# A gated delta rule with the two heads of a block as one 128x128 diagonal tile

## What is computed

```
def gated_delta_rule(q, k, v, beta, log_a):        # chunks of 64 tokens
    g = cumsum(log_a)                              # in the chunk
    a_mat = einsum("bhnid,bhnjd->bhnij", k_beta, k) * decay_strict
    t_inv = triangular_solve(eye + a_mat, eye)     # 64x64, lower
    u = t_inv @ (v * beta)
    w = t_inv @ (k_beta * exp(g))
    p = einsum("bhnid,bhnjd->bhnij", q, k) * decay_causal
    def step(state, xs):                           # chunk after chunk
        v_new = u_c - w_c @ state
        o = q_c @ state + p_c @ v_new
        state = state * exp(gl) + k_c.T @ v_new
```

## Time and profile before

| | before |
|---|---|
| median of 3 runs | 2759.77 us (2758.72 to 2763.18) |
| the profiled execution, its time | 2764.25 us |
| its span, first to last instruction | 2762.5 us |
| mean granted TensorE clock | 0.983 of full speed |
| TensorE busy | 2626.0 us (95%) |
| VectorE busy | 1878.4 us (68%) |
| ScalarE busy | 1232.8 us (45%) |
| GpSimd busy | 405.4 us (15%) |

### The profile page before, as it was taken

The page is one execution under the profiler, slowest core; times in us unless marked ns, Lnnn a source line. Parts: engine busy times, 40 slices in busy tenths (PEclk is TensorE's granted clock), DMA queues, the critical chain, the costliest instruction groups (busy, mean ns, idle before and its releaser), DMA issues.

```text
span 2762.5 us, 38277 instructions
## 1 busy us (share of the span) xinstructions
PE 2626.0 (95%) x15010; PEld 2122.1 (77%) x15010; DVE 1878.4 (68%) x2273; ACT 1232.8 (45%) x2308; POOL 405.4 (15%) x354
## 2 busy tenths in 40 slices
PE   7999998999899999999999999899997999999997
PEld 6887566877788887888778888655776888888885
DVE  3466554673877778888964664589646655578889
ACT  3323565333777763333553334467317433333332
POOL 4322001448200000000300000001374000000002
PEclk9999999999999999999999999899999999999998
DMA  3210000004265655222423223501353232342323
GB/s 136 54 38 13 11 6 24 3 32 183 93 205 188 212 171 193 105 92 107 152 83 116 77 77 122 187 28 35 97 189 125 89 122 92 122 173 101 122 107 122
DMA packets 213484, 290.43 MB, mean 105 GB/s; under 512 B 16551, under 2 KB 143806, under 8 KB 213310
## 3 DMA queue, kind: packets, MB, share of 16 engines
q1 hardware_dynamic: 195918, 227.75, 24.8%
q10 hardware_dynamic: 17392, 60.30, 5.5%
HBM read 220.91 MB, written 67.11 MB: 104 GB/s over the span
## 4 chain that ended last, share of the span: by engine, by line
PE 77%; DVE 11%; ACT 4%; POOL 3%; issue 3%; DMA 2%; SPq 0%; ACTq 0%; DVEq 0%; POOLq 0%
PE ps L1727 7%; PE ps L1728 7%; PE ps L1729 7%; PE ps L1782 6%; PE ps L1784 6%; PE ps L1783 6%; PE ps L1865 4%; PE ps L1866 4%; PE ps L1867 4%; PE ps L1530 2%; PE ps L1436 2%; PE ps L1309 1%; PE ps L1311 1%; PE ps L1310 1%; PE ps L1458 1%
## 5 line engine op out<-in xcount | busy, mean ns | idle before, releaser
L1782 PE MATMUL ps<-down_t_hi,down_s_hi 128*128 128x512 f32 x896 | 349.4, 390 | 3.9 <-DVE acc L3328 2.2
L1784 PE MATMUL ps<-down_t_hi,down_s_lo 128*128 128x512 f32 x896 | 348.6, 389 | 0.0
L1783 PE MATMUL ps<-down_t_lo,down_s_hi 128*128 128x512 f32 x896 | 348.6, 389 | 0.0
L2470 ACT CAST down_s_hi<-down_a 128x2048 fp32r<-128x2048 f32 x56 | 107.3, 1915 | 368.8 <-PE ps L1784 327.1
L1142 POOL TENSOR_SCALAR mean_sq<-ssq 128x1 f32<-128x1 f32 x64 | 37.2, 581 | 1295.8 <-ACT squares_junk_ffn L2018 1246.0
L1727 PE MATMUL ps<-act_hi,up_hi 128*128 128x512 f32 (+1 forms) x544 | 205.7, 378 | 6.1 <-issue 3.6
L1728 PE MATMUL ps<-act_lo,up_hi 128*128 128x512 f32 (+1 forms) x544 | 204.9, 377 | 0.0
L1729 PE MATMUL ps<-act_hi,up_lo 128*128 128x512 f32 (+1 forms) x544 | 204.8, 376 | 0.0
L1782 PEld LDWEIGHTS ps<-down_t_hi,down_s_hi 128*128 128x128 f32 x896 | 168.2, 188 | 41.9 <-issue 7.5
L1784 PEld LDWEIGHTS ps<-down_t_hi,down_s_lo 128*128 128x128 f32 x896 | 168.2, 188 | 35.3
L1783 PEld LDWEIGHTS ps<-down_t_lo,down_s_hi 128*128 128x128 f32 x896 | 168.2, 188 | 34.6
(11 more groups left out here) (382 smaller groups left out, 6460.8 us busy)
## 6 DMA issues: line engine op xcount, KB each, us to landing
down_a<-hid_spill SPq DMA_DIRECT2D x32, 1024.0 KB, 6.6
hid_spill<-up_hid ACTq DMA_DIRECT2D x30, 1024.0 KB, 6.0
w_ada<-in_w_ada SPq DMA_DIRECT2D x48, 512.0 KB, 3.8
up_raw<-in_w_in SPq DMA_DIRECT2D x18, 1024.0 KB, 5.2
raw<-in_w_out SPq DMA_DIRECT2D x32, 512.0 KB, 3.7
up_raw<-in_w_up SPq DMA_DIRECT2D x16, 1024.0 KB, 5.3
down_b<-in_w_down SPq DMA_DIRECT2D x16, 1024.0 KB, 6.7
up_raw<-in_w_mlp_in SPq DMA_DIRECT2D x16, 1024.0 KB, 5.3
```

The source lines that it names most:

```text
L1782: pe.matmul(out, ops["s_hi"][:, k, cols], ops["t_hi"][:, k, :], start=first, stop=False, skip_group_check=True)
L1783: pe.matmul(out, ops["s_hi"][:, k, cols], ops["t_lo"][:, k, :], start=False, stop=False, skip_group_check=True)
L1784: mm = pe.matmul(out, ops["s_lo"][:, k, cols], ops["t_hi"][:, k, :], start=False, stop=last, skip_group_check=True)
```

## The change

The level matrices, the copied Y, `p_T` and `k_dec` are kept as diagonal tiles: [128, 4 blocks, 2, 64] (for `k_dec` two tiles, one for each g), in which the half of the partitions of head g is filled in the columns of g alone and the rest is zero. A matmul with such a tile as weights, 128x128, does both heads at once (`diagonal_products`: 4 matmuls in place of 8). The zeros are written once, by memsets on VectorE before the first level; each later use writes only the filled parts, so what wrote 128 partitions in one instruction now does it in two of 64 (the copy of Y, `p_T`, `k_dec`) or, on GpSimd, in two whole ones with a mask for each g over only the odd blocks of the level, half of the columns. Each level has its own `a_level` tiles. The subtraction of levels 1 to 4 now goes to `t_inv_T`, and the transpose that makes `t_inv` stands right behind it. The constants grow by five masks of 64 columns. The squares for the norm go to `o_normed` in place of a tile of their own.

```diff
@@ constants
+        level = ((k[:, :CHUNK] // s) % 2 == 1) & (r % CHUNK // s == k[:, :CHUNK] // s - 1)
+        for g in range(2 if n else 1):
+            c[:, level_mask(n, g):level_mask(n, g) + CHUNK] = level & (r // CHUNK == g) if n else level
@@ GpSimd, gdn_levels
-                    pool.tensor_tensor(m_s[(n + i) % 2][a][:], a_t[i % 2][a][:], each_block(C_LEVEL + n * CHUNK), ALU.mult)\
-                        .then_inc(sem("level_done"), 1)
+                    if i == 0:
+                        pool.wait_ge(sem("diag_zeroed"), n if n == 1 else n + 1)
+                    for g in range(2):
+                        mask = odd_blocks(consts[:, level_mask(n, g):level_mask(n, g) + CHUNK].unsqueeze(1), n)
+                        ins = pool.tensor_tensor(odd_blocks(m_s[n - 1][a][:, :, g, :], n), odd_blocks(a_t[i % 2][a][:], n),
+                                                 mask.broadcast_to([P, GDN_BLOCKS, CHUNK // LEVELS[n] // 2, LEVELS[n]]), ALU.mult)
+                    ins.then_inc(sem("level_done"), 1)
@@ TensorE
+            def diagonal_products(bank, lhs, rhs, signal):
+                for n in range(GDN_BLOCKS):
+                    mm = pe.matmul(ps[:, bank, n * CHUNK:(n + 1) * CHUNK], lhs[:, n, :, :].rearrange("p g t -> p (g t)"),
+                                   rhs[:, n, :], start=True, stop=True)
+                mm.then_inc(sem(signal), 1)
@@ TensorE, gdn_state_update
-                        for g, m in ((0, 0), (1, 1), (0, 1), (1, 0)):
-                            mm = pe.matmul(ps[gdn_half(m), 5 + g, h * P:(h + 1) * P], k_d[a][gdn_half(g), 2 * h + c, gdn_half(m)],
-                                           v_n[gdn_half(g), h, :], start=True, stop=True)
+                        for g in range(2):
+                            mm = pe.matmul(ps[:, 5 + g, h * P:(h + 1) * P], k_d[a][g][:, 2 * h + c, :], v_n[:, h, :],
+                                           start=True, stop=True)
...
-                    for g in range(2):
-                        n = 2 * h + c
-                        mm = pe.matmul(ps[gdn_half(g), 7, n * P:(n + 1) * P], p_t[a][gdn_half(g), n, :],
-                                       v_n[gdn_half(g), h, :], start=True, stop=True)
+                    n = 2 * h + c
+                    mm = pe.matmul(ps[:, 7, n * P:(n + 1) * P], p_t[a][:, n, :, :].rearrange("p g t -> p (g t)"), v_n[:, h, :],
+                                   start=True, stop=True)
@@ TensorE, gdn_pair
-                            pe.wait_ge(sem("t_done"), 8 * i + (2 * (n - 2) + a + 1))
-                        block_products(a, lambda h, c, rows, b: m_s[(n + i) % 2][a][rows, b, :],
-                                       lambda h, c, rows, b: t_f[f_old][a][rows, b, :], CHUNK, "y_prod")
+                            pe.wait_ge(sem("tr_done"), 8 * i + (2 * (n - 2) + a + 1))
+                        diagonal_products(a, m_s[n - 1][a], t_f[f_old][a], "y_prod")
...
+                        diagonal_products(a if last else 2 + a, y_s[a], t_r[old][a], "zt_prod" if last else "z_prod")
@@ ScalarE, gdn_pair
-                        act.copy(y_s[a][:], block_bank(a)).then_inc(sem("y_done"), 1)
+                        if i == 0 and n == 1:
+                            act.wait_ge(sem("diag_zeroed"), 2)
+                        for g in range(2):
+                            ins = act.copy(y_s[a][gdn_half(g), :, g, :], block_bank(a)[gdn_half(g), :, :])
+                        ins.then_inc(sem("y_done"), 1)
@@ VectorE, gdn_scaled
-                dve.tensor_tensor(p_t[a][:], block_bank(6), e_d[i % 2][a][:], ALU.mult).then_inc(sem("gdn_turn_read"), 1)
+                for g in range(2):
+                    ins = dve.tensor_tensor(p_t[a][gdn_half(g), :, g, :], block_bank(6)[gdn_half(g), :, :],
+                                            e_d[i % 2][a][gdn_half(g), :, :], ALU.mult)
+                ins.then_inc(sem("gdn_turn_read"), 1)
...
-                dve.tensor_tensor(k_d[a][:], bank(4), by_block(G_CD, t), ALU.mult).then_inc(sem("gdn_turn_read"), 1)
+                for g in range(2):
+                    ins = dve.tensor_tensor(k_d[a][g][gdn_half(g), :, :], bank(4)[gdn_half(g), :, :],
+                                            by_block(G_CD, t)[gdn_half(g), :, :], ALU.mult)
+                ins.then_inc(sem("gdn_turn_read"), 1)
@@ VectorE, before the first pair
             dve.memset(state[0][:], 0.0).then_inc(sem("state_done"), 1)
+            gdn_system(0, 0)
+            zeroed(m_s[0])
+            gdn_first_turn(0, 0)
+            gdn_system(0, 1)
+            gdn_first_turn(0, 1)
+            zeroed(y_s)
+            for n in range(1, 5):
+                zeroed(m_s[n])
+            dve.memset(p_t[0][:], 0.0)
+            dve.memset(p_t[1][:], 0.0)
             for a in range(2):
-                gdn_system(0, a)
-                gdn_first_turn(0, a)
+                for g in range(2):
+                    dve.memset(k_d[a][g][:], 0.0)
```

More of the change, by code:

```diff
@@ L354, with level_mask @@
 C_LEVEL = 640
-C_ID64 = C_LEVEL + CHUNK * len(LEVELS)
+C_ID64 = C_LEVEL + CHUNK * (2 * len(LEVELS) - 1)
 C_CSUM64 = C_ID64 + CHUNK
+def level_mask(n, g):
+    return C_LEVEL + CHUNK * (2 * n - 1 + g if n else 0)
 C_KEYCAP = C_CSUM64 + CHUNK
@@ L613, in blocks, with diagonal @@
             return [sb(f"{name}{a}", kb + a, [P, GDN_BLOCKS, CHUNK]) for a in range(2)]
[L615 to L618, removed]
+        k_w, v_b, u_s, w_t, o_i = (tile_pair(n, kb) for n, kb in (
+            ("k_w", 25), ("v_b", 29), ("u", 41), ("w_T", 45), ("o_inter", 53)))
+        k_d = [[head_tile(f"k_dec{a}_{g}", kb) for g, kb in enumerate(kbs)] for a, kbs in enumerate(((49, 51), (189.25, 194)))]
+        def diagonal(name, kb):
+            return sb(name, kb, [P, GDN_BLOCKS, 2, CHUNK])
+        e_d, a_t, t_f = ([blocks(f"{n}{x}_", kb + 2 * x) for x in range(2)]
+                         for n, kb in (("decay", 89), ("a_T", 93), ("t_inv", 101)))
+        m_s = [[diagonal(f"a_level{n + 1}_{a}", kb) for a, kb in enumerate(kbs)]
+               for n, kbs in enumerate(((33, 35), (37, 39), (97, 99), (67, 69), (71, 185)))]
         t_r = [blocks(f"t_inv_T{x}_", 105 + 2 * x) for x in range(3)]
-        y_s, p_t = blocks("level_y", 111), blocks("p_T", 113)
+        y_s = [diagonal(f"level_y{a}", 111 + 2 * a) for a in range(2)]
+        p_t = [diagonal(f"p_T{a}", 199 + 2 * a) for a in range(2)]
         def t_home(i):
@@ L631, in two_blocks @@
         v_n = sb("v_new", 119, [P, 2, P])
-        s_dec, o_s, o_sq, o_n = (head_tile(n, kb) for n, kb in (
-            ("state_dec", 187), ("o_tok", 192), ("o_sq", 194), ("o_normed", 196)))
+        s_dec, o_s, o_n = (head_tile(n, kb) for n, kb in (("state_dec", 187), ("o_tok", 192), ("o_normed", 196)))
         e_last = sb("exp_g_last", 204.5, [P, NT, 2, GDN_HEADS])
@@ L1177, in each_block, with odd_blocks @@
                 return consts[:, mask:mask + CHUNK].unsqueeze(1).broadcast_to([P, GDN_BLOCKS, CHUNK])
+            def odd_blocks(block, n):
+                return block.rearrange("p b (q two s) -> p b q two s", two=2, s=LEVELS[n])[:, :, :, 1, :]
             def gdn_levels(i, n):
@@ L2210, in gdn_squares @@
                 for n in range(GDN_BLOCKS):
-                    ins = act.activation(o_sq[:, n, :], o_s[:, n, :], ACT.Square, accum_out=o_ss[:, n:n + 1])
+                    ins = act.activation(o_n[:, n, :], o_s[:, n, :], ACT.Square, accum_out=o_ss[:, n:n + 1])
                 ins.then_inc(sem("o_ss_done"), 1)
@@ L2976, in gdn_level_turn @@
                 dve.wait_ge(sem("t_done"), 8 * i + (2 * (n - 1) + a + 1))
-                dve.transpose(t_r[t_slot(i, n)][a][:].rearrange("p n t -> p (n t)"), t_f[(n + i) % 2][a][:].rearrange("p n t -> p (n t)"))\
+                dve.transpose(t_f[(n + i) % 2][a][:].rearrange("p n t -> p (n t)"), t_r[t_slot(i, n)][a][:].rearrange("p n t -> p (n t)"))\
                     .then_inc(sem("tr_done"), 1)
@@ L3028, in gdn_pair @@
                 for n in range(1, len(LEVELS)):
-                    old, new, f_new, last = t_slot(i, n - 1), t_slot(i, n), (n + i) % 2, n == len(LEVELS) - 1
+                    old, new, last = t_slot(i, n - 1), t_slot(i, n), n == len(LEVELS) - 1
                     if i and not last:
@@ L3046, in gdn_pair @@
                             dve.wait_ge(sem("z_prod"), 8 * i + (2 * (n - 1) + a + 1))
-                            dve.tensor_tensor(t_f[f_new][a][:], t_f[1 - f_new][a][:], block_bank(2 + a), ALU.subtract)\
+                            dve.tensor_tensor(t_r[new][a][:], t_r[old][a][:], block_bank(2 + a), ALU.subtract)\
                                 .then_inc(sem("t_done"), 1)
+                            gdn_level_turn(i, n, a)
                     for a in range(2):
-                        if not last:
-                            gdn_level_turn(i, n, a)
-                        elif more:
+                        if last and more:
                             gdn_first_turn(i + 1, a)
@@ L3059, in gdn_pair, with zeroed @@
```

(10 more changed lines are left out.)

10 lines of the change are left out of this document (removed).

## The result

The changed kernel takes 2819.31 us, the median of 4 runs (2816.7 to 2834.32), and the kernel before on the same chip 2760.64 us (2758.72 to 2763.18, 4 runs). The ratio is 1.0221, with a 95% interval of 1.0206 to 1.0235: slower, as forecast, but by 59 us and not by 37, and above the range.

What follows compares the result with a forecast made beforehand. TensorE was taken to bound the later pairs, a chain of dependent work the first. Terms 25.0 + 6.5 + 2.0 + 2.2 + 0.7 + 0.4 = 36.8 us gave 2797 us against the median; eight-in-ten range 2780 to 2814.

Steps and rivals of the forecast that it cites:

- the last of the first pair: First pair's low clock: one level at 1.2 GHz, +2.8 us, taken as +2, bounds 0 and 8.
- the chain shows; or the clock stays low: Rival, 17%: later pairs' copies or subtraction and transpose uncovered, or first pair's clock low; 2803 to 2812, say 2807 us.
- my 106: Price in ns of a joined 128x128 pass, set by its weight load, with the stream overlapped.
- levels +7.7 us a pair for +6.4: Levels 1 to 4 of a later pair: level products 1.25 and state update 0.36 a level, +6.4 us on TensorE.
- The end of a pair: `gdn_scaled` on VectorE: p_T and k_dec in two, plus dependent transposes, +2.0 us, bounds 1.3 and 2.8.
- The series rival: Rival, 6%: a joined pass's load and stream follow one another, 160 ns a pass; 2832 us.
- the cheap pass: Rival, 5%: a joined pass costs no more than a small one, 32 ns; 2758 us, not slower.
- much is absorbed: Rival, 12%: TensorE's idle time swallows part, memsets run beside waits, low clock goes away; 2787, at the least 2781 us.
- The memsets: First pair: 18 on VectorE ahead of the first level subtraction, putting it at about 484.4, +6.5 us.
- The copies: Copies of Y in two parts, 0.8 us a tile; in later pairs hidden under y of tile 1 and the update.
- The tail: Last chunks' state waits for L1573's longer state update, two of them uncovered: +0.7 us.
- the +4.2 predicted: First pair behind the first subtraction: its end's +2.2 us, with +2 for the clock among them.

Runs made afterwards that it cites:

- idle matmuls in the waits: Changed kernel plus ten fp32 matmuls with unused results where TensorE waits in the first pair: runs 2804.59 to 2830.06 us, ratio 1.0207.
- small tiles: Changed kernel with the first pair's level products alone made by 64x64 weights again: 2817.28 us, ratio 1.019.
- wider streams: Changed kernel with three of the four joined level products of a tile streaming 128 columns instead of 64: 2810.68 us, ratio 1.0173.
- the kernel with late memsets: Changed kernel with 12 of its 18 memsets moved behind the transposes of levels 1 to 4 of the first pair: 2814.55 us, ratio 1.019.

## Why the prediction was wrong

**The step that failed** is the last of the first pair: "At 1.2 GHz a level is 4 x 1.7 = 6.8 us: one such level costs +2.8, which I take as +2, bounds 0 and 8." The price of a level at 1.2 GHz was right (3.4 us a product, 6.8 a level), the count of such levels was not. I took the kernel before as the model, in which the clock came back a few microseconds after the wait, and assumed that TensorE's work would bring it back here too. With joined products it did not in four levels and the most of the fifth, some 44 us where it had been 10: 57.55 us against 47.7 with idle matmuls in the waits, so 9.9 us or more for my 2, and beyond the bound of 8. Three kernels with the same memsets show that what TensorE executes makes the difference: with small tiles (45.3 us), wider streams (46.3) and filled waits (47.7) the clock came back within the pair, though in each it was at half for 7 to 14 us. Which property of the joined products keeps it down is not shown. My rival "the chain shows; or the clock stays low" named this and gave it too small a price, 2803 to 2812, and too small a chance.

**Mis-sized.** A pass was 114 to 115 ns for my 106, and 119 for the state update: levels +7.7 us a pair for +6.4. The earlier trace rows give the load's price with one column streamed; under 64 and 128 columns it is 8 to 12% dearer. The end of a pair was +2.5 for +2.0: a write of half the partitions took 0.44 and 0.70 us from start to start, a whole instruction's own duration, where I had used the whole one's spacing of 0.33 and 0.60. Together 1.8 us a pair, 5.5 in three.

**Missing.** That behind the longer wait at a pair's end the clock falls in some executions, for 5.7 us in a middle pair with joined products and 4.6 to 9.9 in the last. It isn't in the profiled run of the changed kernel, and so not in the table of stages; its run of 2834.32 us had a mean clock of 0.972 against 0.979. That such falls lengthen it is not seen in that run itself; it is argued from the scatter that shrank and from the long run of the kernel with late memsets, whose trace shows two of them and 10 us.

**Base.** The prediction took the profiled run's 4.5 us above the median off again; the profiled run of after lay 2.0 us below its own. Of the 22.8 us between the sum and the measured median that is 6.5, and the stages are 16.3.

**Right.** The direction and its cause: two small tiles ran side by side, and joining them saves nothing, since a pass of 128 weight columns costs over three small ones. The series rival falls by the wide streams, the cheap pass by 115 ns, "much is absorbed" by the stages. The memsets: +7.1 for +6.5, the first subtraction 1.5 us later than the 484.4 given. The copies (0.82 us a tile for 0.8) and transposes are covered, but for 0.19 us before level 5, where it was 0.23 before the change; GpSimd's masks took 0.42 us each, less than the 0.60 allowed, at no price. The tail, +0.7, did not come. That the first pair with idle matmuls grew by +4.1 behind the first subtraction, as the +4.2 predicted, is luck in part: both hold some of the clock, my +2 and its 7 us at half, and the +2.2 for the pair's end alone was not measured apart.

## What to carry to other kernels

Before two matmuls on different parts of the array are joined, look whether they already run side by side: compare the time from start to start with that of one over the whole array. Where full-height products are wanted, split them by weight columns (at most 34 ns for each half here, 115 for the whole). When a change lengthens a wait of TensorE, price not only the wait but what the work behind it costs at half clock, for as long as the rows of the nearest stage don't show that work bringing the clock back; and read the scatter of the runs, since one profiled run can miss it.

## What was unexpected of the hardware

TensorE was busy 4.00 of 4 us at a granted clock of 0.50 or 0.51 over more than 20 us, from 490 to 518, and got the full clock only behind other products, which began at 513. The same weights with wider streams took no longer a pass (114 ns) and had the full clock from 492 to the end of the pair. And idle matmuls that lengthen a middle pair by 0.4 us and the last by 1.1 made a kernel 11 us faster.
